# U's first four operands asked for between the two halves of W2's first rows

## The reference

```
for l in range(DEPTH):
    ...                                    # norm, mixers, output projection, residual
    h2 = _rmsnorm(x, norm2_g[l])
    x = x + jnp.square(jax.nn.relu(h2 @ w_ff1[l])) @ w_ff2[l]     # w_ff1: 1024 x 4096, w_ff2: 4096 x 1024
```

## Time and profile before

| | |
|---|---|
| median of 3 runs | 2113.79 us (2111.49 to 2116.09) |
| profiled execution, its own time | 2116.16 us |
| profiled execution, span of the trace | 2114.4 us |
| busy share of PE, DVE, POOL, ACT | 98%, 64%, 45%, 42% |
| share of PE in the chain that ended last | 92% |

### The profile page before, as it was taken

How to read it: one execution, slowest core, us unless ns; L and a number is a source line. 1 busy time by engine, 2 the same in 40 slices (tenths; PEclk the granted TensorE clock), 3 DMA queues, 4 the chain that set the end, 5 groups by cost and what they waited for, 6 DMA issues and landing times.

```text
span 2114.4 us, 32317 instructions
## 1 busy us (share of the span) xinstructions
PE 2079.4 (98%) x10916; PEld 1739.9 (82%) x10916; DVE 1349.1 (64%) x1646; ACT 879.6 (42%) x1467; POOL 958.0 (45%) x699
## 2 busy tenths in 40 slices
PE   7999999999999999999999999999999999999998
PEld 7888888898888878888888888788988888788886
DVE  5037765487777777676640477754877777767664
ACT  5135453266666632121241444432656666312120
POOL 4235524335445546564541465233245544646452
PEclk9999999999999999999999999999999999999999
DMA  6222245426777799677432223453367777996763
GB/s 216 95 99 80 84 159 158 157 83 201 262 246 240 239 375 364 261 274 286 175 134 95 99 81 114 150 160 128 100 220 242 253 268 250 377 357 241 300 236 147
DMA packets 222800, 423.12 MB, mean 200 GB/s; under 512 B 24296, under 2 KB 158184, under 8 KB 214512
## 3 DMA queue, kind: packets, MB, share of 16 engines
q1 hardware_dynamic: 153808, 347.35, 46.3%
q10 hardware_dynamic: 68896, 74.53, 10.2%
HBM read 268.60 MB, written 153.22 MB: 200 GB/s over the span
## 4 chain that ended last, share of the span: by engine, by line
PE 92%; DVE 3%; DMA 2%; issue 1%; SPq 1%; POOL 0%; ACT 0%; ACTq 0%; DVEq 0%; POOLq 0%
PE ps L1828 26%; PE ps L1779 24%; PE ps L1547 13%; PE ps L1477 9%; PE ps L1638 8%; PE ps L1457 4%; DMA uk<-uD 1%; PE ps L1448 1%; PE ps L1599 1%; PE ps L1586 1%; PE ps L1572 1%; PE ps L1680 1%; PE ps L1689 1%; DMA sel<-in_selector 1%; DVE tS L2330 1%
## 5 line engine op out<-in xcount | busy, mean ns | idle before, releaser
L1828 PE MATMUL ps<-w2s,uk 128*128 128x512 f32 x2688 | 612.4, 390 | 3.6 <-DMA uk<-uD 2.5
L1828 PEld LDWEIGHTS ps<-w2s,uk 128*128 128x128 f32 x2688 | 503.5, 188 | 111.6 <-DMA uk<-uD 3.7
L2342 DVE TENSOR_TENSOR xs<-ps,xs 128x1024 f32<-128x1024 f32 x208 | 253.8, 1221 | 183.4 <-PE ps L1828 180.7
L1779 PE MATMUL ps<-hT,w1s 128*128 128x512 f32 x1344 | 313.9, 389 | 0.0
L1399 POOL TENSOR_TENSOR w2s<-raw,w2s 128x1024 fp32r<-128x1024 f32 x64 | 187.1, 2937 | 250.3 <-ACT w2s L1166 250.3
L1779 PEld LDWEIGHTS ps<-hT,w1s 128*128 128x128 f32 x1344 | 252.1, 188 | 53.0 <-issue 0.8
L1395 POOL TENSOR_TENSOR w1s<-rawf,w1s 128x512 fp32r<-128x512 f32 x112 | 150.0, 1350 | 217.1 <-ACT w1s L1047 217.1
L1547 PE MATMUL ps<-hT,whi 128*128 128x512 f32 x768 | 242.0, 396 | 0.0
L1779 PE MATMUL ps<-tT,w1s 128*128 128x512 f32 x1008 | 237.5, 389 | 0.4 <-issue 0.4
L1779 PEld LDWEIGHTS ps<-tT,w1s 128*128 128x128 f32 x1008 | 189.1, 188 | 40.4 <-issue 1.2
L1166 ACT CAST w2s<-raw 128x1024 fp32r<-128x1024 f32 x64 | 66.0, 1052 | 363.0 <-PE ps L1828 216.1
(11 more groups left out here) (218 smaller groups left out, 3059.7 us busy)
## 6 DMA issues: line engine op xcount, KB each, us to landing
uk<-uD SPq DMA_DIRECT2D x64, 1024.0 KB, 8.1
raw<-in_wstream SPq DMA_DIRECT2D x100, 512.0 KB, 5.7
uk<-uD SPq DMA_DIRECT2D x64, 768.0 KB, 5.8
rawf<-in_wstream SPq DMA_DIRECT2D x64, 512.0 KB, 4.2
uD<-uh ACTq DMA_DIRECT2D x64, 512.0 KB, 7.0
uD<-uf SPq DMA_DIRECT2D x64, 512.0 KB, 7.7
uD<-uh ACTq DMA_DIRECT2D x64, 384.0 KB, 4.1
uD<-uf SPq DMA_DIRECT2D x64, 384.0 KB, 7.0
```

The source lines that it names most:

```text
L1779: mm = pe.matmul(ps[:, bank, :], w, x[:, k, :], start=(first and k == 0 and i == 0), stop=(k == 3 and i == 2), skip_group_check=True)
L1828: mm = pe.matmul(ps[:, bank + tp, :], u, w2s[r][:, w, k, :], start=(r in (1, 2, 5) and k == 0 and i == 0), stop=(k == 1 and i == 2), skip_ ...
L2342: V.tensor_tensor(y, ps[:, bank:bank + 2, :], y, ALU.add).then_inc(y_acc, 1)
```

## The change

The two loops over `a` in the four requests for W2 of group 0 are taken apart. The blocks a = 0 are asked for where all four were, the blocks a = 1 after the request for the first four operands of U. The requests, their sizes and their number are the same, and no wait of any engine is changed. The requests for the other groups still go through `load_w2`.

```
                 sp.wait_ge(m1_lo, l * FM + FM)
                 alone(sp)
-                load_w2(0)
+                for k in range(2):
+                    sp.dma_start(raw2[:, k, 0, :], wstream[l, UB + UC + 4 * k + 2]).then_inc(m2_raw, 16)
                 sp.wait_ge(f_m, l * FM + FM - 7 + POSZ[2] + 1)
                 alone(sp)
                 sp.wait_ge(u_hst, l * (64 * CH) + 128)
                 alone(sp)
                 sp.wait_ge(u_lst, l * (64 * CH) + 128)
                 alone(sp)
-                load_u(0, 0, 0, None); load_u(0, 0, 1, None)
+                load_u(0, 0, 0, None)
+                for k in range(2):
+                    sp.dma_start(raw2[:, k, 1, :], wstream[l, UB + UC + 4 * k + 3]).then_inc(m2_raw, 16)
+                load_u(0, 0, 1, None)
                 store_ul(LAST, 0)
```

## The result

The changed kernel takes 2124.14 us (median of 4 runs, 2123.63 to 2124.3), the kernel before 2113.18 us in the same comparison: 11.0 us more, a ratio of 1.0053 with a 95% interval of 1.0041 to 1.0065. The profiled execution took 2124.27 us, its span is 2122.5. So the change is slower by more than the 0.2% that can be told.

The account below looks back on a forecast made before the run. PE, busy for 98% of the span, was taken to bound the kernel. Layer 0's 3.85 and layer 1's 4.5 gave +8.4 us on the profiled 2116.16, or 2124.6; less 2.4 for the median, 2122.2 us, range 2117.5 to 2126.0.

Parts of the forecast that it names:

- The forecast case: Phase 2 seams: W2's second halves land 5 us late in both layers, +7.8 to +9.5 us; chance 0.74.
- The start of phase 2: Layer 0 seam: PE, free at 750.97, idles 4.5 us for POOL's first tile and starts at about 755.5.
- The block's shift: First seven products of phase 2: the block ends 5.1 us later in each layer, before waits are won back.
- The clock's fall: Both seams: PE's granted clock falls to 0.50 after the idle time; worth 0.3 us in layer 0, bounds 0 and 1.6.
- What is won back: PE's waits behind phase 2's start vanish: 0.84 and 0.45 us in layer 0, 0.16 and 0.48 in layer 1.
- Landing in between: Rival at the seams: W2's second halves share the line with U's second transfer, land 3.3 us late, +4.5 us; chance 0.10.
- W2 not queueing behind U: Rival at the seams: second halves are served beside U, land 1.3 us late, +0.6 us, no change; chance 0.08.
- A second stall: Rival at group 1: W2, asked for later, lands at 791 and PE waits 2 us in each layer, +12.4; chance 0.08.

Follow-up runs that it names:

- e2: The change with W2's second halves asked for behind only 1 MB of U, against the kernel before: ratio 1.0031, +6.1 us.
- e3: The change with W2's second halves asked for behind U's parts 0 and 1 (3.5 MB), against the kernel before: ratio 1.0088, +19.2 us.
- e9: The kernel before, unchanged, profiled twice more: 2113.42 and 2113.46 us.
- e6: The change with 32 unused transposes of a constant on PE between phase 1 and phase 2, against the kernel before: ratio 1.0054, +10.7 us.
- e0: The kernel before run once more without edit, against the kernel before: ratio 1.0, +0.1 us; its profiled execution took 2117.08 us.

## Why the prediction was right, and what was mis-sized

- **The forecast case came about.** W2's second halves landed when U's part 0 used to, 5.0 us later in layer 0 and 5.3 in layer 1. U came 2.5 us sooner, and nobody needed it. Shown by ACT's wait, and by the series of e2, the change and e3.
- **The start of phase 2** was forecast at 755.5 with 4.5 us of idle time; it is at 756.97 with 4.55 (phase 1 ended 1.45 later in this execution). Over the six seams of the three profiles of the change PE idled 4.33 to 4.96 us. PE follows POOL's first tile.
- **The block's shift.** With 5.1 us a layer it was right: against the first execution of e9, phase 2 of layer 0 is 300.54 - 295.40 = 5.1 us longer, and of layer 1 320.01 - 315.29 = 4.7, or 5.2 with the 0.47 that PE no longer waits behind the start there.
- **The clock's fall** came at both seams. That its price would be far below the 1.6 us that PE loses held in five of six seams of the change, where the traces of e6 put it at 0.0 to 0.1 us and not 0.3. In the sixth the block ended 1.2 us later.
- **What is won back** is the term that was mis-sized: 1.9 us in the sum (0.84 + 0.45 + 0.16 + 0.48), about 0.5 by e9. It was read from one execution that lay 2.4 us above the median, and these were the very waits that made it long. I had put the execution's surplus aside by adding the gain to the median; a part of that surplus stood in the sum as room to be won back. (The first profile was longer than every timed run of before that was known then, not only longer than their median.) With 0.5 the sum is 2 x 5.1 - 0.5 = 9.7 us; the timed runs gave 11.0 with an interval from 8.7 to 13.7. What is left, 1.3 us, lies within the scatter, and no term is shown for it.
- **The rivals.** Landing in between, and W2 not queueing behind U, are excluded by the landing 13.8 us after the first request. A second stall did not come: ACT's wait for W2 of group 1 ended at 785.17, and DVE took its first sum at 789.85, without waiting.
- What made the waits behind the start come in two of the four profiles of before is open. The wait for `uk[1]` came in layer 0 of the first and in layer 1 of e0. There the second transfer of `uk[1]` took 10.0 and 10.2 us from asking to landing; in the other six seams it took 8.0 to 9.3 and PE did not wait. Why it took longer is not shown: it was not varied.

## What to carry to other kernels

When transfers stand in one line, as these did (2.5 us for each MB put ahead), moving one forward moves another back by the same bytes; ask which of the two has work between its landing and the engine that waits. Here W2 had a rounding, a difference and a tile on POOL ahead of PE, 3.5 us, and U had none, so W2 had to stay in front. A count over several transfers makes the first user wait for the last of them, which here made up 6.6 of the 11.0 us. Before a gap in one profiled execution is counted as room that a delay can fill, profile a second execution, above all when the first lies above the median.

## What was not expected of the hardware

Two of four profiled executions of the kernel before had a phase 2 that was 2 us longer than in the other two, most of it in waits behind the starts, though the idle times at the starts differed by 0.5 us at most. The changed kernel, whose PE waits for one late transfer at each seam, stayed within 0.9 us over its six executions (2123.63 to 2124.5), while the kernel before spread over 4.6 in its first three; that the wait is the reason is not shown.

The same fall of the granted clock to 0.50 cost 0.0 to 0.1 us in five seams, because PE was waiting for POOL's tiles, and went with a block 1.2 us longer in the sixth, where the clock was still at 0.57 in the stretch from 4.5 to 5 us behind PE's start.
